# The first two blocks of modulation columns: all of them on TensorE in four banks, instead of three quarters on TensorE and one on VectorE

## The chip, the cores and the metric

One core of a Trainium2 chip runs the whole program in one launch. The metric is the device time in microseconds (us), the median of three runs.

## The reference, cut to what matters

One transformer block over 1024 latent tokens and 256 context tokens of width 1024. Before anything else it computes the modulation from two condition vectors, and it normalizes, scales and shifts every token with it:

```
s_c, s_ctx = silu(c), silu(c_ctx)                 # two vectors of 1024
mx = split(s_c   @ w_mod + b_mod, 6)              # w_mod: 1024 x 6144
mc = split(s_ctx @ w_mod + b_mod, 6)
xn = rms_norm(x,   g) * (1 + mx[1]) + mx[0]       # shift: columns 0..1023
cn = rms_norm(ctx, g) * (1 + mc[1]) + mc[0]       # scale: columns 1024..2047
... = xn @ w_in, cn @ w_in
```

Then follow a recurrence, a neighborhood attention, the merge of both and a gated feed-forward. They use `mx[2]` to `mx[5]`, which are computed later and are not touched here. The change is about columns 0 to 2047 of `w_mod`, that is 16 blocks of 128 columns, for both vectors.

## The kernel before, in words

The program is a row of blocks: `setup_block`, `mixer_block`, `merge_block` and `ffn_block`. Each is one `nc.Block`, and at its end all engines meet, so that nothing of the mixer, not even a transfer, starts before the last engine has left the setup.

Everything is kept with features on the 128 partitions: token data `xs[128, 8, 1280]`, eight chunks k of 128 features by 1280 tokens. The setup does the following.

- **SyncE** (the queue SP) issues the transfers in one written order: small ones, then the sixteen transfers of the tokens, then eight pieces of `w_mod` (`load_wm(k)`, L188, 128 x 1536 numbers each, into a ring of four, so that piece k waits for `wm_used` of piece k-4), among which stand the silu source `sr` (L196), four row blocks `load_rows(b)` (L193, ring of two) and weight tiles `raw` (L203, L205, L211, L214). The last two `raw` loads wait for `w_lo`.
- **VectorE** adds the squares of the tokens (L352), then (L354) takes them off TensorE's sums; GpSimd raises them to the power -0.5 (L223); three small operations on VectorE (L358 to L360) finish 1/rms and signal `rstd_done`.
- **TensorE** sums the squares (L232), and then computes the columns: `columns(k)` (L236 to L241) multiplies chunk k of the silu vectors `sv` (2 stationary columns) with three pieces of 512 columns, and accumulates over the eight k in three PSUM banks. After `columns(1)` it waits for `rstd_done` and spreads 1/rms over the partitions by ten transposes (L248, signal `spread`). After `columns(7)` ScalarE copies the two rows of results to `mrow` (L287), and TensorE turns them to 12 columns (L253, signal `mod_cols`).
- The three pieces are columns 0 to 511 of the shift and all 1024 of the scale. The other 512 columns of the shift are **row dots**: `shift_dots(b)` (L315, L317) on VectorE multiplies 128 transposed rows of `w_mod` by the silu vectors, which lie spread over all partitions in `sr` (loaded spread by L196, silu on ScalarE by L281), and sums along the row. The four calls stand between the steps of 1/rms, the four `normalize(k)` (L328, which waits for `spread`) and two `split_low(s)` (L325). L371 adds the bias to them.
- After `mod_cols` VectorE makes the scale `gm` (L375, L376), adds the bias to the first half of the shift (L378), and then, chunk by chunk, scales and shifts the tokens (L386, L389); ScalarE makes the high part `xnh` (L291, L293, L294), VectorE the low part `xnl` (L396, L400), signal `lo_done`. TensorE follows chunk by chunk with the first matmuls of the projection (L262 to L264), fifteen for each chunk.

The lines that say what a sentence can't:

```
for k in range(KC):
    columns(k)
    if k == 1:
        pe.wait_ge(rstd_done, 1)
        ... ten transposes, then_inc(spread, 1)
pe.wait_ge(mod_copied, 1)
```

Of the kernel before, what the change touches and what calls it, by code (L numbers as in the profile page):

```python
# [9 lines left out]
ALU = mybir.AluOpType  # L10
ACT = mybir.ActivationFunctionType
AX_X = mybir.AxisListType.X

P = 128
D = 1024
KC = D // P
# [16 lines left out]
HALF = 512  # L33
# [19 lines left out]

def build(nc, xT, ctxT, svec, c_rows, w_modk, w_shiftT, w_modT, b_mod, gains, w_fm, w_qkv, lru_w, lru_p, qk_g, rpb,
          w_mix, w_ff, ffn_p, consts, outT, yr_d, yn_d, smr_d, smn_d, bias_d):
    with ExitStack() as top:
# [10 lines left out]
        mod = sbuf(top, "mod", [P, 6 * KC, 2])  # L67
# [14 lines left out]
        with ExitStack() as queries:  # L82
            qh = sbuf(queries, "qh", [P, KC, 384], F32R)
            ql = sbuf(queries, "ql", [P, KC, 384], F32R)
        setup_block(nc, sem, sbuf, psum, xT, ctxT, svec, c_rows, w_modk, w_shiftT, gains, b_mod, lru_p, consts, w_fm, w_qkv,
                    mod, bm, gain, ones, eps, lrup, decay, xnh, xnl, qh, ql, weights, banks)
# [19 lines left out]
SEGS = ((0, C), (C, C + HALF), (C + HALF, N))  # L106
MOD_COLS = 1536
MOD_RING = 4
ROW_BLOCKS = 4
SCALED_EARLY = 4  # L110


def setup_block(nc, sem, sbuf, psum, xT, ctxT, svec, c_rows, w_modk, w_shiftT, gains, b_mod, lru_p, consts, w_fm, w_qkv,
                mod, bm, gain, ones, eps, lrup, decay, xnh, xnl, qh, ql, weights, banks):
# [5 lines left out]
    with ExitStack() as st:  # L120
# [3 lines left out]
        total = sbuf(st, "total", [P, N])  # L124
        rows = sbuf(st, "rows", [P, 2, D])
        product = sbuf(st, "product", [P, D])
        sv = sbuf(st, "sv", [P, KC, 2])
        sr = sbuf(st, "sr", [P, 2, D])
        dots = sbuf(st, "dots", [P, ROW_BLOCKS, 2])
        gm = sbuf(st, "gm", [P, 2, KC])  # L130
        la = sbuf(st, "la", [P, 6, 2, KC])
        ident = sbuf(st, "ident", [P, P])
        mrow = sbuf(st, "mrow", [P, 3, HALF])
        rms = sbuf(st, "rms", [P, 3, TB])
# [3 lines left out]
        ga = acc[:, 3, :]  # L138
        gf = gf[:, :]
        mt = ga[:, 0:24].rearrange("p (n w) -> p n w", w=2)  # L140
        ss = gf[:, 0:TB]
        rs = lower[:, 0:N]

        small_in = sem("a_small_in")
        sr_in = sem("a_sr_in")
        x_in = [sem(f"a_x_in{k}") for k in range(KC)]
        wm_in = [sem(f"a_wm_in{s}") for s in range(MOD_RING)]
        wm_used = sem("a_wm_used")
        rows_in = [sem(f"a_rows_in{s}") for s in range(2)]
        rows_used = sem("a_rows_used")  # L150
        memset_done = sem("a_memset")
        silu_done = sem("a_silu")
        sr_done = sem("a_sr_done")
        squared = sem("a_squared")
# [18 lines left out]
        with nc.Block() as block:  # L173
            @block.sync
            def _(sp):
                sp.dma_start(sv[:, :, :], svec).then_inc(small_in, 16)
                sp.dma_start(bm[:, :], b_mod).then_inc(small_in, 16)
                sp.dma_start(gain[:, :, :], gains).then_inc(small_in, 16)
                sp.dma_start(lrup[:, :, :], lru_p).then_inc(small_in, 16)
                sp.dma_start(ident[:, :], consts[:, 0:P]).then_inc(small_in, 16)  # L180
                for k in range(KC):
                    sp.dma_start(xs[:, k, 0:C], ctxT[k]).then_inc(x_in[k], 16)
                    sp.dma_start(xs[:, k, C:N], xT[k]).then_inc(x_in[k], 16)

                def load_wm(k):
                    if k >= MOD_RING:
                        sp.wait_ge(wm_used, k - MOD_RING + 1)
                    sp.dma_start(wm[:, k % MOD_RING, :], w_modk[k]).then_inc(wm_in[k % MOD_RING], 16)  # L188

                def load_rows(b):  # L190
                    if b >= 2:
                        sp.wait_ge(rows_used, b - 1)
                    sp.dma_start(rows[:, b % 2, :], w_shiftT[b]).then_inc(rows_in[b % 2], 16)  # L193

                load_wm(0)
                sp.dma_start(sr[:, :, :], bass.AP(tensor=c_rows.tensor, offset=0, ap=[[0, P], [D, 2], [1, D]]))\  # L196
                  .then_inc(sr_in, 16)
                load_wm(1)
                load_rows(0)
                load_wm(2)  # L200
                load_rows(1)
                load_wm(3)
                sp.dma_start(raw[:, 0, :], w_fm[0, :, 0:1024]).then_inc(raw_in[0], 16)  # L203
                load_wm(4)
                sp.dma_start(raw[:, 1, :], w_fm[0, :, 1024:2048]).then_inc(raw_in[1], 16)  # L205
                load_wm(5)
                load_rows(2)
                load_wm(6)
                load_rows(3)
                load_wm(7)  # L210
                sp.dma_start(raw[:, 2, :], w_qkv[0, :, 2048:3072]).then_inc(raw_in[2], 16)  # L211
                for s in range(2):
                    sp.wait_ge(w_lo, s + 1)
                    sp.dma_start(raw[:, s, :], w_qkv[0, :, 1024 * s:1024 * s + 1024]).then_inc(raw_in[s], 16)  # L214
# [12 lines left out]
            def _(pe):  # L227
# [8 lines left out]
                def columns(k):  # L236
                    pe.wait_ge(wm_in[k % MOD_RING], (k // MOD_RING + 1) * 16)
                    for n in range(3):
                        last = pe.matmul(acc[0:2, n, :], sv[:, k, :], wm[:, k % MOD_RING, HALF * n:HALF * n + HALF],
                                         start=(k == 0), stop=(k == KC - 1))  # L240
                    last.then_inc(wm_used, 1)  # L241
# [9 lines left out]
                pe.wait_ge(mod_copied, 1)  # L251
                for n in range(12):
                    last = pe.transpose(mt[:, n, :], mrow[0:2, n // 4, P * (n % 4):P * (n % 4) + P], ident[0:2, 0:2])  # L253
# [13 lines left out]
            def _(act):  # L267
# [4 lines left out]
                for k in range(KC):  # L272
# [6 lines left out]
                    act.activation(sq[:, k % 2, :], xs[:, k, :], ACT.Square).then_inc(squared, 1)  # L279
                act.wait_ge(sr_in, 16)  # L280
                act.activation(sr[:, :, :], sr[:, :, :], ACT.Silu).then_inc(sr_done, 1)  # L281
                for s in range(2):
# [3 lines left out]
                act.wait_ge(wm_used, KC)  # L286
                act.copy(mrow[0:2, :, :], acc[0:2, 0:3, :]).then_inc(mod_copied, 1)  # L287
                for k in range(KC):
# [12 lines left out]
            def _(dve):  # L301
                steps = [0]

                def then(ins):

                    steps[0] += 1
                    ins.then_inc(dve_step, 1)
                    dve.wait_ge(dve_step, steps[0])

                def shift_dots(b):  # L310

                    dve.wait_ge(rows_in[b % 2], (b // 2 + 1) * 16)
                    if b == 0:
                        dve.wait_ge(sr_done, 1)
                    dve.tensor_tensor_reduce(out=product[:, :], in0=rows[:, b % 2, :], in1=sr[:, 0, :], scale=1.0,  # L315
                                             scalar=0.0, op0=ALU.mult, op1=ALU.add, accum_out=dots[:, b, 0:1])
                    dve.tensor_tensor_reduce(out=rows[:, b % 2, :], in0=rows[:, b % 2, :], in1=sr[:, 1, :],  # L317
                                             scale=1.0, scalar=0.0, op0=ALU.mult, op1=ALU.add,
                                             accum_out=dots[:, b, 1:2]).then_inc(rows_used, 1)
                    dve.wait_ge(rows_used, b + 1)  # L320

# [26 lines left out]
                for k in range(1, KC):  # L348
                    dve.wait_ge(squared, k + 1)
                    if k >= 2:  # L350
# [3 lines left out]
                dve.tensor_scalar(rms[:, 0, :], ss, 1.0 / D, EPS, ALU.mult, ALU.add).then_inc(mean_square, 1)  # L354
                shift_dots(0)
                dve.wait_ge(root_done, 1)
# [3 lines left out]
                dve.scalar_tensor_tensor(r, w, 1.5, r, ALU.add, ALU.mult).then_inc(rstd_done, 1)  # L360
                shift_dots(1)
                dve.wait_ge(spread, 1)
# [3 lines left out]
                split_low(1)  # L366
                shift_dots(2)
                normalize(2)
                shift_dots(3)
                normalize(3)  # L370
                then(dve.tensor_tensor(mod[:, 4:KC, :], dots[:, :, :],  # L371
                                       bm[:, 4:KC].unsqueeze(2).broadcast_to([P, 4, 2]), ALU.add))
                dve.wait_ge(mod_cols, 1)
                for w in range(2):
                    then(dve.tensor_tensor(gm[:, w, :], mt[:, 4:12, w], bm[:, KC:2 * KC], ALU.add))  # L375
                    then(dve.scalar_tensor_tensor(gm[:, w, :], gm[:, w, :], 1.0, gain[:, 0, :],  # L376
                                                  ALU.add, ALU.mult))
                then(dve.tensor_tensor(mod[:, 0:4, :], mt[:, 0:4, :],  # L378
                                       bm[:, 0:4].unsqueeze(2).broadcast_to([P, 4, 2]), ALU.add))

# [1676 lines left out]
```

## Time and profile before

| | |
|---|---|
| runs | 2293.88, 2295.71, 2296.64 us; median 2295.71 |
| the profiled execution, its own time | 2292.44 us |
| its span | 2290.7 us, 29048 instructions |
| TensorE matmul busy | 2152.3 us (94%) |
| VectorE busy | 1407.6 us (61%) |
| ScalarE busy | 955.9 us (42%) |
| GpSimd busy | 263.7 us (12%) |
| mean bandwidth to and from HBM | 74 GB/s |

The profile shows one execution. The span is the time between the first and the last instruction that it shows; 1.74 us of the execution's own time lie around it. An f32 matmul is shown as two records (an instruction with 512 columns stands there twice), an fp32r one as one. The engine names are PE (matmul), PEld (weight load), DVE (VectorE), ACT (ScalarE), POOL (GpSimd) and SP (SyncE), and SPq is the issuing of a transfer on SP.

### The profile page before, as it was taken

What the parts mean: (1) busy time and instruction counts of PE and PEld (TensorE: products, weight loads), DVE (VectorE), ACT (ScalarE), POOL (GpSimd) and SP (SyncE); (2) the same over time, 40 slices, a digit from 0 to 9 for tenths busy, and PEclk for the clock granted to TensorE, in tenths of its full rate; (3) what the DMA queues carried; (4) which work ended last, traced back from release to release, by engine and by line L of the source; (5) the groups of instructions that cost most, each with busy time, mean ns of one, the idle gap of its engine ahead of it and who ended that gap; (6) DMA issues with size and microseconds to landing.
All of it is one profiled execution on the core that took longest, in us unless ns stands there. A gap on an engine that the chain in (4) does not pass through costs nothing. (4 is left out here: it accounts for less than half of the span.)

```text
span 2290.7 us, 29048 instructions
## 1 busy us (share of the span) xinstructions
PE 2152.3 (94%) x10958; PEld 1824.1 (80%) x10958; DVE 1407.6 (61%) x2572; ACT 955.9 (42%) x1472; POOL 263.7 (12%) x202
## 2 busy tenths in 40 slices
PE   5988999999999999999987799997999999999999
PEld 1877888978789788897876688875888888888887
DVE  6678587775886858768578446657554244424442
ACT  3556655665657556566557210104221022212220
POOL 0031222112212113022221100000000000000000
PEclk9999999999999999999999899998999999999999
DMA  7411212011120111111102544421221111111112
GB/s 305 119 46 36 67 38 77 28 38 59 46 68 19 54 60 37 38 58 49 56 19 88 207 165 139 152 91 69 73 70 58 48 46 53 47 55 47 53 48 99
DMA packets 68632, 167.56 MB, mean 73 GB/s; under 512 B 22704, under 2 KB 28208, under 8 KB 68400
## 3 DMA queue, kind: packets, MB, share of 16 engines
q1 hardware_dynamic: 47520, 145.20, 18.6%
q0 software_dynamic: 4608, 16.78, 2.1%
q10 hardware_dynamic: 16400, 4.19, 0.9%
q8 instruction: 66, 1.08, 0.2%
q14 instruction: 38, 0.31, 0.0%
HBM read 145.17 MB, written 25.17 MB: 74 GB/s over the span
## 5 line engine op out<-in xcount | busy, mean ns | idle before, releaser
L48 PE MATMUL t_o_ps<-qh,xnh 128*128 128x384 f32 (+1 forms) x640 | 223.5, 349 | 0.3 <-PEq L173 0.3
L50 PE MATMUL t_o_ps<-qh,xnl 128*128 128x384 f32 (+1 forms) x640 | 207.6, 324 | 0.0
L49 PE MATMUL t_o_ps<-ql,xnh 128*128 128x384 f32 (+1 forms) x640 | 207.6, 324 | 0.0
L1383 DVE TENSOR_TENSOR probT_low<-t_o_ps,probT_high 128x512 fp32r<-128x512 f32 (+2 forms) x256 | 138.9, 584 | 64.8 <-ACT probT_high L1086 64.1
L806 PE MATMUL f_ps<-xnh,wh 128*128 128x512 f32 x360 | 151.5, 421 | 11.8 <-DVE wl L1214 9.3
L1086 ACT CAST probT_high<-t_o_ps 128x512 fp32r<-128x512 f32 (+2 forms) x256 | 117.0, 510 | 92.3 <-PE t_o_ps L897 71.2
L1843 ACT CAST wh<-raw 128x1024 fp32r<-128x1024 f32 x68 | 70.9, 1044 | 192.0 <-PE pd L50 170.1
L807 PE MATMUL f_ps<-xnl,wh 128*128 128x512 f32 x360 | 143.1, 397 | 0.0
L808 PE MATMUL f_ps<-xnh,wl 128*128 128x512 f32 x360 | 143.0, 397 | 0.0
L50 PE MATMUL pg<-yh,wl 128*128 128x512 f32 x352 | 137.0, 389 | 0.0
L49 PE MATMUL pg<-yl,wh 128*128 128x512 f32 x352 | 137.0, 389 | 0.0
L48 PE MATMUL pg<-yh,wh 128*128 128x512 f32 x352 | 137.0, 389 | 0.0
L50 PE MATMUL pa<-yh,wl 128*128 128x512 f32 x336 | 130.8, 389 | 0.0
L48 PE MATMUL pa<-yh,wh 128*128 128x512 f32 x336 | 130.8, 389 | 0.0
L49 PE MATMUL pa<-yl,wh 128*128 128x512 f32 x336 | 130.8, 389 | 0.0
L1076 ACT ACTIVATE prob<-prob,stat 128x768 f32<-128x768 f32 (+1 forms) x128 | 128.1, 1001 | 3.8 <-DVE stat L1378 3.8
L1965 DVE SCALAR_TENSOR_TENSOR x<-pd,mod,x 128x512 f32 (+1 forms) x48 | 35.8, 750 | 151.3 <-PE pd L50 146.6
L48 PEld LDWEIGHTS t_o_ps<-qh,xnh 128*128 128x128 f32 x640 | 120.8, 189 | 9.0 <-issue 8.3
L49 PEld LDWEIGHTS t_o_ps<-ql,xnh 128*128 128x128 f32 x640 | 120.8, 189 | 8.3 <-issue 7.6
L1257 DVE TENSOR_REDUCE ssq<-sqs 128x4 f32<-128x256 f32 (+1 forms) x80 | 31.0, 389 | 150.0 <-ACT sqs L1032 149.7
L50 PEld LDWEIGHTS t_o_ps<-qh,xnl 128*128 128x128 f32 x640 | 120.7, 189 | 0.0
L48 PE MATMUL pd<-hh_d,wh 128*128 128x512 f32 x308 | 119.9, 389 | 0.0
(311 smaller groups left out, 5640.6 us busy)
## 6 DMA issues: line engine op xcount, KB each, us to landing
raw<-w_ff SPq DMA_DIRECT2D x68, 512.0 KB, 3.2
raw<-w_fm SPq DMA_DIRECT2D x32, 512.0 KB, 6.5
raw<-w_qkv SPq DMA_DIRECT2D x24, 512.0 KB, 3.6
raw<-w_mix SPq DMA_DIRECT2D x24, 512.0 KB, 4.4
bias<-bias_d SPq DMA_DIRECT2D x16, 448.0 KB, 5.7
wm<-w_modk SPq DMA_DIRECT2D x8, 768.0 KB, 7.7
row_c<-w_modT SPq DMA_DIRECT2D x12, 512.0 KB, 3.2
raw<-w_modT SPq DMA_DIRECT2D x12, 512.0 KB, 3.3
```

Of the source, the lines that this page charges most:

```text
L48: pe.matmul(out, w_hi(k), x_hi(k), start=(k == 0), stop=False)
L49: pe.matmul(out, w_hi(k), x_lo(k), start=False, stop=False)
L50: last = pe.matmul(out, w_lo(k), x_hi(k), start=False, stop=(k == chunks - 1))
L806: pe.matmul(out, fh[:, s, k, :], xnh[:, k, c0:c1], start=(k == 0), stop=False)
L807: pe.matmul(out, fh[:, s, k, :], xnl[:, k, c0:c1], start=False, stop=False)
L808: return pe.matmul(out, fl[:, s, k, :], xnh[:, k, c0:c1], start=False, stop=(k == KC - 1))
L1076: act.activation(p, p, ACT.Exp, bias=stat[:, u, 1:2], scale=-1.0, accum_out=stat[:, u, 2:3]).then_inc(exp_done, 1)
L1086: act.copy(probT_blocks(pth, u, bank), probT_bank(u, bank)).then_inc(pt_hi, 1)
L1257: dve.tensor_reduce(ssq[:, s, g0:4], sqs[:, s % 2, HD * g0:256].rearrange("p (g f) -> p g f", f=HD), AX_X, ALU.add).then_inc(sq_used, 1)
L1383: dve.tensor_tensor(probT_blocks(ptl, u, bank), probT_bank(u, bank), probT_blocks(pth, u, bank).bitcast(F32), ALU.subtract).then_inc(pt_lo, 1)
L1843: act.copy(flat(wh, b), raw[:, b, :]).then_inc(w_hi, 1)
L1965: dve.scalar_tensor_tensor(out, pd[:, 2 * b + half, :], mod[:, bass.ds(m + 5 * KC, 1), 0:1].rearrange("p a b -> p (a b)"), out, ALU.mult, ...
```

## The change

All 2048 columns of the two blocks go through TensorE. A piece of `w_mod` is 128 x 2048 numbers, `columns(k)` has four matmuls into four banks, `mrow` has four rows of 512, there are 16 transposes, and they go to another bank (the one of the sums of squares). The row dots, their four transfers, the spread silu source, its transfer and its silu on ScalarE, and L371 are gone. On the host, `w_modk` is a plain slice and `w_shiftT` is no more.

```diff
-MOD_COLS = 1536
+MOD_COLS = 2048
 MOD_RING = 4
-ROW_BLOCKS = 4
...
-        mrow = sbuf(st, "mrow", [P, 3, HALF])
+        mrow = sbuf(st, "mrow", [P, 4, HALF])
...
-        mt = ga[:, 0:24].rearrange("p (n w) -> p n w", w=2)
+        mt = gf[:, 64:96].rearrange("p (n w) -> p n w", w=2)
...
                 load_wm(0)
-                sp.dma_start(sr[:, :, :], bass.AP(tensor=c_rows.tensor, offset=0, ap=[[0, P], [D, 2], [1, D]]))\
-                  .then_inc(sr_in, 16)
                 load_wm(1)
-                load_rows(0)
                 load_wm(2)
-                load_rows(1)
                 load_wm(3)
                 sp.dma_start(raw[:, 0, :], w_fm[0, :, 0:1024]).then_inc(raw_in[0], 16)
                 load_wm(4)
                 sp.dma_start(raw[:, 1, :], w_fm[0, :, 1024:2048]).then_inc(raw_in[1], 16)
                 load_wm(5)
-                load_rows(2)
                 load_wm(6)
-                load_rows(3)
                 load_wm(7)
...
                     pe.wait_ge(wm_in[k % MOD_RING], (k // MOD_RING + 1) * 16)
-                    for n in range(3):
+                    for n in range(4):
...
                 pe.wait_ge(mod_copied, 1)
-                for n in range(12):
+                for n in range(16):
...
-                act.wait_ge(sr_in, 16)
-                act.activation(sr[:, :, :], sr[:, :, :], ACT.Silu).then_inc(sr_done, 1)
...
-                act.copy(mrow[0:2, :, :], acc[0:2, 0:3, :]).then_inc(mod_copied, 1)
+                act.copy(mrow[0:2, :, :], acc[0:2, :, :]).then_inc(mod_copied, 1)
...
-                shift_dots(0)
                 dve.wait_ge(root_done, 1)
...
                 dve.scalar_tensor_tensor(r, w, 1.5, r, ALU.add, ALU.mult).then_inc(rstd_done, 1)
-                shift_dots(1)
                 dve.wait_ge(spread, 1)
                 normalize(0)
                 split_low(0)
                 normalize(1)
                 split_low(1)
-                shift_dots(2)
                 normalize(2)
-                shift_dots(3)
                 normalize(3)
-                then(dve.tensor_tensor(mod[:, 4:KC, :], dots[:, :, :],
-                                       bm[:, 4:KC].unsqueeze(2).broadcast_to([P, 4, 2]), ALU.add))
                 dve.wait_ge(mod_cols, 1)
                 for w in range(2):
-                    then(dve.tensor_tensor(gm[:, w, :], mt[:, 4:12, w], bm[:, KC:2 * KC], ALU.add))
+                    then(dve.tensor_tensor(gm[:, w, :], mt[:, 8:16, w], bm[:, KC:2 * KC], ALU.add))
...
-                then(dve.tensor_tensor(mod[:, 0:4, :], mt[:, 0:4, :],
-                                       bm[:, 0:4].unsqueeze(2).broadcast_to([P, 4, 2]), ALU.add))
+                then(dve.tensor_tensor(mod[:, 0:KC, :], mt[:, 0:KC, :],
+                                       bm[:, 0:KC].unsqueeze(2).broadcast_to([P, KC, 2]), ALU.add))
```

## Rows read from the trace of the kernel before

**Rows 1.** The page: busy time of the engines over the whole span
```profile
PE 2152.3 (94%) x10958; PEld 1824.1 (80%) x10958; DVE 1407.6 (61%) x2572; ACT 955.9 (42%) x1472; POOL 263.7 (12%) x202
```
**Rows 2.** Waits, 0 to 60 us: who waited for whom, total, times, longest
```profile
ACT mrow L287 <- PE s_ps L239: 12.3, 1, 12.3
...
DVE gm L375 <- PE s_ps L253: 4.6, 1, 4.6
```
**Rows 3.** Timeline: start, length, engine, operation; TensorE from the sums on
```profile
27.49 7.73 PE L239 MATMUL s_ps<-wm,sv 128*2 128x512 f32 x12
...
29.16 0.13 PEld L239 LDWEIGHTS s_ps<-wm,sv 128*2 128x2 f32 x1 [0.73 <-issue]
30.01 0.13 PEld L239 LDWEIGHTS s_ps<-wm,sv 128*2 128x2 f32 x1 [0.73 <-issue]
...
35.15 1.31 PE L248 MATMUL t_o_ps<-ident,rms 128*128 128x128 f32 x10
...
36.38 15.61 PE L239 MATMUL s_ps<-wm,sv 128*2 128x512 f32 x36
```
**Rows 4.** The same timeline: from the end of the columns to the first projection
```profile
52.03 1.43 ACT L287 COPY mrow<-s_ps 2x1536 f32<-2x1536 f32 x1 [12.28 <-PE s_ps L239]
...
53.52 0.90 PE L253 MATMUL s_ps<-ident,mrow 2*128 2x2 f32 x12 [1.52 <-ACT mrow L287]
54.52 0.17 DVE L375 TENSOR_TENSOR gm<-s_ps,bm 128x8 f32<-128x8 f32 x1 [4.61 <-PE s_ps L253]
...
59.63 0.55 PE L262 MATMUL s_ps<-xnh,wh 128*128 128x256 f32 x1 [5.21 <-DVE xnl L396]
```
**Rows 5.** Timeline of VectorE: 1/rms, the first normalize, the last step before `mod_cols`
```profile
31.30 0.17 DVE L360 SCALAR_TENSOR_TENSOR rms<-rms 128x10 f32<-128x10 f32 x1
...
36.56 1.49 DVE L328 TENSOR_TENSOR xs<-xs,t_o_ps 128x1280 f32<-128x1280 f32 x1 [2.80 <-PE t_o_ps L248]
38.08 1.23 DVE L325 TENSOR_TENSOR wl<-raw,wh 128x1024 fp32r<-128x1024 f32 x1
...
49.75 0.17 DVE L371 TENSOR_TENSOR mod<-dots,bm 128x8 f32<-128x8 f32 x1
```
**Rows 6.** Timeline: the mixer's first matmul, and what released it
```profile
86.56 0.36 PE L48 MATMUL t_o_ps<-qh,xnh 128*128 128x256 f32 x1 [0.30 <-PEq L173]
```
**Rows 7.** Groups by line and shape, 0 to 60 us: busy us, mean ns, idle before
```profile
L291 ACT CAST xnh<-xs 128x1280 fp32r<-128x1280 f32 x2 | 2.4, 1257 | 3.2 <-DVE xs L386 3.2
L284 ACT CAST wh<-raw 128x1024 fp32r<-128x1024 f32 x2 | 2.1, 1045 | 11.3 <-DMA raw<-w_fm 11.3
```
**Rows 8.** The same groups: the row dots and the spread silu
```profile
L315 DVE CUSTOM_DVE_ANT_0 product<-rows,sr 128x1024 f32<-128x1024 f32 x4 | 4.9, 1222 | 0.0
L317 DVE CUSTOM_DVE_ANT_0 rows<-rows,sr 128x1024 f32<-128x1024 f32 x4 | 4.9, 1220 | 0.0
...
L281 ACT ACTIVATE sr<-sr 128x2048 f32<-128x2048 f32 x1 | 1.9, 1910 | 1.8 <-DMA sr<-c_rows 1.8
```
**Rows 9.** Timeline of SP: when transfers of the ring are issued
```profile
32.67 0.33 SPq L188 DMA_DIRECT2D wm<-w_modk  x1
...
42.10 0.43 SPq L211 DMA_DIRECT2D raw<-w_qkv  x1
42.57 1.04 SPq L214 DMA_DIRECT2D raw<-w_qkv  x2
```
**Rows 10.** Stretch: length, busy PE, PEld, DVE, ACT, POOL, PEclk, DMA share, GB/s
```profile
44.00:48.00 4.00, 4.00 (x11) 0.80 (x10) 3.93 (x6) 0.00 (x0) 0.00 (x0) 1.00 1.02 421
```
**Rows 11.** Stretches by L262 alone: first two chunks of the projection, length first
```profile
59.60:64.42 4.82, 2.67 (x6) 1.65 (x6) 0.64 0.01 3
64.42:67.50 3.08, 1.84 (x5) 0.94 (x5) 1.00 0.00 0
```
**Rows 12.** Timeline: distance of fp32r matmuls of 512 columns in the projection
```profile
65.00 0.39 PE L263 MATMUL s_ps<-xnl,wh 128*128 128x512 f32 x1
65.23 0.39 PE L264 MATMUL s_ps<-xnh,wl 128*128 128x512 f32 x1
```

More of the change, by code:

```diff
@@ L51, in three_passes, with build @@
     return last
-def build(nc, xT, ctxT, svec, c_rows, w_modk, w_shiftT, w_modT, b_mod, gains, w_fm, w_qkv, lru_w, lru_p, qk_g, rpb,
+def build(nc, xT, ctxT, svec, c_rows, w_modk, w_modT, b_mod, gains, w_fm, w_qkv, lru_w, lru_p, qk_g, rpb,
           w_mix, w_ff, ffn_p, consts, outT, yr_d, yn_d, smr_d, smn_d, bias_d):
@@ L84, in build @@
             ql = sbuf(queries, "ql", [P, KC, 384], F32R)
-        setup_block(nc, sem, sbuf, psum, xT, ctxT, svec, c_rows, w_modk, w_shiftT, gains, b_mod, lru_p, consts, w_fm, w_qkv,
+        setup_block(nc, sem, sbuf, psum, xT, ctxT, svec, c_rows, w_modk, gains, b_mod, lru_p, consts, w_fm, w_qkv,
                     mod, bm, gain, ones, eps, lrup, decay, xnh, xnl, qh, ql, weights, banks)
@@ L106, with setup_block @@
 SEGS = ((0, C), (C, C + HALF), (C + HALF, N))
-MOD_COLS = 1536
+MOD_COLS = 2048
 MOD_RING = 4
-ROW_BLOCKS = 4
 SCALED_EARLY = 4
-def setup_block(nc, sem, sbuf, psum, xT, ctxT, svec, c_rows, w_modk, w_shiftT, gains, b_mod, lru_p, consts, w_fm, w_qkv,
+def setup_block(nc, sem, sbuf, psum, xT, ctxT, svec, c_rows, w_modk, gains, b_mod, lru_p, consts, w_fm, w_qkv,
                 mod, bm, gain, ones, eps, lrup, decay, xnh, xnl, qh, ql, weights, banks):
@@ L124, in setup_block @@
         total = sbuf(st, "total", [P, N])
-        rows = sbuf(st, "rows", [P, 2, D])
-        product = sbuf(st, "product", [P, D])
         sv = sbuf(st, "sv", [P, KC, 2])
-        sr = sbuf(st, "sr", [P, 2, D])
-        dots = sbuf(st, "dots", [P, ROW_BLOCKS, 2])
         gm = sbuf(st, "gm", [P, 2, KC])
@@ L144, in setup_block @@
         small_in = sem("a_small_in")
-        sr_in = sem("a_sr_in")
         x_in = [sem(f"a_x_in{k}") for k in range(KC)]
@@ L148, in setup_block @@
         wm_used = sem("a_wm_used")
-        rows_in = [sem(f"a_rows_in{s}") for s in range(2)]
-        rows_used = sem("a_rows_used")
         memset_done = sem("a_memset")
         silu_done = sem("a_silu")
-        sr_done = sem("a_sr_done")
         squared = sem("a_squared")
@@ L188, in load_wm @@
                     sp.dma_start(wm[:, k % MOD_RING, :], w_modk[k]).then_inc(wm_in[k % MOD_RING], 16)
[L190 to L193, printed above, removed]
                 load_wm(0)
-                sp.dma_start(sr[:, :, :], bass.AP(tensor=c_rows.tensor, offset=0, ap=[[0, P], [D, 2], [1, D]]))\
-                  .then_inc(sr_in, 16)
                 load_wm(1)
-                load_rows(0)
                 load_wm(2)
-                load_rows(1)
                 load_wm(3)
@@ L308, in then @@
                     dve.wait_ge(dve_step, steps[0])
[L310 to L320, printed above, removed]
                 def split_low(s):
@@ L2035 @@
         "svec": np.stack([cols(a["c"][0]), cols(a["c_ctx"])], 2),
-        "c_rows": np.stack([a["c"][0], a["c_ctx"]]), "w_modk": np.concatenate([a["w_mod"][0][:, 0:HALF], a["w_mod"][0][:, D:2 * D]], 1).reshape(KC, P, MOD_COLS),
-        "w_shiftT": a["w_mod"][0][:, HALF:D].T.reshape(ROW_BLOCKS, P, D),
+        "c_rows": np.stack([a["c"][0], a["c_ctx"]]), "w_modk": a["w_mod"][0][:, 0:MOD_COLS].reshape(KC, P, MOD_COLS),
         "w_modT": a["w_mod"][0][:, 2 * D:].T.reshape(4 * KC, P, D), "b_mod": cols(a["b_mod"][0]),
```

## The prediction

> **What bounds the kernel now.** I read the busy times first: TensorE is busy for 94% of the span and no other engine for more than 61% [rows 1]. So work that is added to TensorE costs its length wherever TensorE is what the others wait for, and work that is taken from VectorE gives nothing there. That is an average over stages, and the change lies in the first 60 us; the second view is therefore the list of waits of this stretch. The longest waits after the token sums point one way: ScalarE's copy to `mrow` stood 12.3 us waiting for the columns, and VectorE's first operation on them, L375, stood 4.6 us waiting for the transposes [rows 2]. The third view, the timeline, gives the path that sets the end of the setup: columns from 27.49 us, ten transposes at 35.15, columns again from 36.38 for 15.61 us [rows 3], the copy at 52.03, the turning at 53.52, VectorE at 54.52, the projection at 59.63, after 5.2 us of waiting for the first chunk of tokens, which itself waits for the columns [rows 4]. VectorE had ended its last work before that, L371, at 49.75 + 0.17 = 49.92 us [rows 5]: it had 4.6 us to spare. Last, the mixer's first matmul comes at 86.56 us, released by the end of the block (L173) [rows 6], where all engines meet. Whatever delays the columns delays the whole rest by the same.
>
> **What the change costs on that path.**
> *The matmuls.* Eight chunks get one f32 matmul of 512 columns more, 16 records. In the second stretch 36 records take 15.61 us, 0.434 each with the last one's tail, so I take 0.43 [rows 3]. In the first chunk the distance of two weight loads is 30.01 - 29.16 = 0.85 us, twice that: TensorE then runs at the lower of its two levels. The first twelve records take 7.66 us (27.49 to 35.15) [rows 3]; with s slow ones 0.85s + 0.43(12 - s) = 7.66, so s is about 6. The start at 27.49 hangs on the token sums, which the change leaves alone, so I let the slow stretch be as long in time as before: six records slow in either kernel. The first two chunks then take 7.66 + 4 x 0.43 = 9.4 us and the others 12 x 0.43 = 5.2 us more than before: together **+6.9 us**. Bounds: below, no f32 record stands closer than 0.43 (what if one could is rival 2); above, all 16 at 0.85 would be 13.6, but when twelve of them come the stream has long been fast, so I take as the upper end that the four of the first two chunks are slow, 6.9 + 4 x 0.42 = 8.6.
>
> That the price per matmul is the moving columns' and not an overlap that a fourth bank would fill rests on that row alone. The Trainium skill, "TensorE: Matmul & The Clock Gate", section "Back-to-back issue gap", gives some 131 ns as the sustained distance of matmuls of 512 columns, and "FP8 and Floating Point Precision" counts four passes for true FP32: by these an instruction would be 0.52 us, the eight would cost 4.2 us, and the sum below would be 4.9. The trace disagrees: 0.87 us for an instruction of two records.
>
> *ScalarE's copy* has 2048 instead of 1536 numbers in a row. A cast of 1280 takes 1.257 us and one of 1024 1.045 [rows 7], 0.83 ns a number, so 512 more are **+0.43**. The nearest bound above is in proportion, 1.43/3 = 0.48 [rows 4]; below I see 0.35 if a fixed part is larger than it seems. It lies on the path.
>
> *The turning.* Twelve transposes take 0.90 us [rows 4], four more about a third of it less the fixed part, **+0.25** (0.2 to 0.3). That they go to the bank of the sums of squares costs nothing: VectorE has read them before it makes 1/rms, and the projection writes it only after VectorE has read the columns.
>
> *VectorE after them.* L378 has 16 numbers instead of 8. Its like L375 takes 0.17 us with 8 [rows 4]; between nothing and in proportion (0.17) I take **+0.02**, since so short an operation is nearly all fixed time. L375 and L376 stay.
>
> Sum on the path: 6.9 + 0.43 + 0.25 + 0.02 = **+7.6 us**.
>
> **What is removed, and why it gives nothing.** The row dots are 4 x 1.222 + 4 x 1.220 = 9.8 us on VectorE, with the reads of their accumulators and L371 some 10.6 [rows 8]. The first call runs while GpSimd makes the root; without it VectorE waits for the root at the same time as before. 1/rms would be ready at 31.5 us as before [rows 5], but TensorE asks for it only after two chunks, now at 27.49 + 9.4 = 36.9 instead of 35.15. So `spread` and the first `normalize` come 1.7 us *later*, at 38.3. Then four normalizes (1.49) and two splits (1.23) [rows 5] end at about 38.3 + 8.4 = 46.7, if the second weight tile is there; `mod_cols` comes at about 54.4 + 7.6 = 62.0. VectorE's spare time grows from 4.6 to some 15 us. The silu on ScalarE, 1.9 us and its table [rows 8], stands between the squares and a cast of a weight tile that stood waiting for its transfer (L284, 11.3 us in two waits [rows 7]): also beside the path. If these covers were gone, the removed work would be worth those 10.6 us; nothing is near it.
>
> **The queue and the transfers.** Gone are the spread source (1.0 MB) and four row blocks (2.1 MB), added is 8 x 0.26 = 2.1 MB. Before 27 us the tokens' transfers stand first in the queue, so the start does not move. The ring: piece 4 can be issued when the first chunk is used, at 27.5 + 6 x 0.85 + 2 x 0.43 = 33.4 instead of 32.67 [rows 9], piece 5 at 36.9, 6 at 41.5, 7 at 44.9. TensorE wants piece 4 at 44.9 (two chunks of 3.44 us after the transposes' end at 38.1) and piece 7 at 55.2, 10.3 us after its issue. Behind piece 7 three weight tiles are issued at once (0.52 MB each) [rows 9]; even if all share the 421 GB/s that this time shows [rows 10], 2.6 MB are in after 6.2 us, and 4 us are left for the way there. So the ring costs nothing. What waits behind the later `load_wm` on SP are those three tiles; ScalarE wants them only after all token chunks, so behind 59.63 [rows 4]. The chunk loop after `mod_cols` is the same work with the same data and shifts whole.
>
> **The rivals.**
> 1. *The clock.* TensorE rests while the copy and the first chunk are made, and comes back slow: the first chunk of the projection takes 4.82 us at a granted 0.64, the next 3.08 at 1.00 [rows 11], so this drop costs 1.7 us; the slow start at 27.49 costs 6 x 0.42 = 2.5. If the rise comes at another moment of the stream, either can be smaller or larger: the sum becomes 7.6 - 4.2 = +3.4 at the least, and as far the other way 7.6 + 4.2 = +11.8, that is 2299.1 to 2307.5. For it speaks that these rows show both levels; against it, that start and gaps are the same in both kernels and a median over runs meets the same lottery: the runs before lie within 2.8 us. The Trainium skill, "TensorE: Matmul & The Clock Gate", section "What's actually happening", says that the number of slow matmuls at a start differs from run to run, 6, 11 or 14 in one kernel; no run here shows that yet. Chance 0.12, half of it small enough for "within 0.2%".
> 2. *The fourth matmul is partly free*, because matmuls into one more bank overlap more. The shortest distance that rows show for 512 columns is that of fp32r ones in the projection, 65.23 - 65.00 = 0.23 us [rows 12]; at that distance 16 records are 3.7 us, and the sum is 3.7 + 0.7 = +4.4, 2300.1. Against it: 36 f32 records, over three banks, without a hole at 0.43. The rule of the Trainium skill quoted above (TensorE: Matmul & The Clock Gate) points this way, and the row speaks against it. Chance 0.02.
> 3. *Vector work was the real bound* (faster). If the dots delayed what TensorE or ScalarE waits for, 10.6 us go and only the copy and the turning (+0.7) come: -9.9 us, 2285.8. It decides from the point where VectorE's last operation before L375 ends after `mod_cols`; the trace has it 4.6 us ahead. The same sign, smaller, if the columns started earlier for the 1 MB less in the queue; but they start behind the token sums. Chance 0.02.
> 4. *The ring starves TensorE.* A piece is a third larger and three tiles share its way. If pieces 4 to 7 came 1 us late each, +4 to the sum, +11.6, 2307.3, just outside the range. It decides from 10.3 us between issue and landing. Chance 0.04.
> 5. *The edit gives no change*, some wait in the mixer swallowing the shift. Its engines all start together, so there is no slack to swallow it: 2295.7. Chance 0.02.
>
> **How the numbers follow.** The profiled execution took 2292.44 us (span 2290.7, 1.74 around it), so with the change it would take 2300.0. It was the fastest one shown; the median is 3.27 us above it, and the same sum against the median gives 2295.71 + 7.6 = **2303.3 us**, +0.33%. My forecast has a chance of 0.78. A measurement of this kernel can tell 0.2% from no change, 4.6 us. "Within" gets half of rival 1, rivals 2 and 5 in part, and the forecast's own scatter: 0.11; faster 0.02; slower 0.87. The range goes down to +3.8 and up to +11.3, nearly the ends of rival 1, with the bounds of the terms inside: 2299.5 to 2307.0.
>
> **What would show it.** In the profile after: 64 records of L239 at 0.43 us; transposes L248 at about 36.9; the copy at about 58.9 with 1.86 us; 16 transposes in 1.15 to 1.2; L375 at about 62.1 with a wait of 14 to 16 us on TensorE; the first L262 at about 67.2, the mixer at 94.1. The prediction is wrong if the copy starts before 57 or after 61, if TensorE waits for a transfer of `wm`, or if the mixer's start has moved by 7.6 us and the end has not.

## The result, and the profile after

The changed kernel takes **2302.07 us** (median of nine runs, 2300.78 to 2303.53), the kernel before 2294.38 us in as many (2293.64 to 2296.64): +7.7 us, a ratio of 1.0031 with an interval of 1.0022 to 1.0041, so clearly slower, by 5 to 9 us. The forecast was +7.6 us; the 2303.3 us are 1.2 us too high, since the median of three runs that they start from was itself 1.3 us above that of nine.

The busy times of the page after. TensorE has 8 us more, VectorE 11 us less, ScalarE 2 us less [rows 1]:

```profile
PE 2160.4 (94%) x10978; PEld 1827.4 (79%) x10978; DVE 1396.5 (61%) x2555; ACT 953.8 (41%) x1470; POOL 262.1 (11%) x202
```

The waits of the first 70 us after (who waited for whom, total, times, longest). The copy waits 18.1 us for the columns instead of 12.3, VectorE 15.5 us for the turning instead of 4.6 [rows 2]. All that VectorE no longer has to do has become waiting:

```profile
ACT mrow L265 <- PE s_ps L219: 18.1, 1, 18.1
...
DVE gm L335 <- PE f_ps L233: 15.5, 1, 15.5
DVE xs L294 <- PE t_o_ps L228: 6.6, 1, 6.6
```

The path after, in the timeline (start, length, engine, operation), to lay beside [rows 3], [rows 4] and [rows 6]:

```profile
27.09 8.34 PE L219 MATMUL s_ps<-wm,sv 128*2 128x512 f32 x16
35.37 1.31 PE L228 MATMUL t_o_ps<-ident,rms 128*128 128x128 f32 x10
36.60 20.76 PE L219 MATMUL s_ps<-wm,sv 128*2 128x512 f32 x48
...
57.40 1.85 ACT L265 COPY mrow<-s_ps 2x2048 f32<-2x2048 f32 x1 [18.07 <-PE s_ps L219]
...
59.31 1.15 PE L233 MATMUL f_ps<-ident,mrow 2*128 2x2 f32 x16 [1.95 <-ACT mrow L265]
60.56 0.17 DVE L335 TENSOR_TENSOR gm<-f_ps,bm 128x8 f32<-128x8 f32 x1 [15.53 <-PE f_ps L233]
...
65.68 0.55 PE L242 MATMUL s_ps<-xnh,wh 128*128 128x256 f32 x1 [5.22 <-DVE xnl L356]
...
93.32 0.33 SPq L588 DMA_DIRECT2D cst<-consts  x1
```

48 records take 20.76 us where 36 took 15.61, 0.43 each in both. The mixer's first transfer, the end of the setup, is at 93.32 us. In the kernel before it is 6.8 us earlier:

```profile
86.51 0.33 SPq L628 DMA_DIRECT2D cst<-consts  x1
```

### The profile page after: what moved, and what is told of

It is laid out like the page before. It is cut to its first block and busy times, and to the rows that moved or that the text cites. A ratio compares the mean times of both kernels' runs of the same rounds, so it can differ in the third digit from the quotient of the medians.

```text
span 2299.0 us, 29060 instructions
## 1 busy us (share of the span) xinstructions
PE 2160.4 (94%) x10978; PEld 1827.4 (79%) x10978; DVE 1396.5 (61%) x2555; ACT 953.8 (41%) x1470; POOL 262.1 (11%) x202
```

## The experiments

All kernels keep the mixer and everything behind it. "Rest" below is the time from the mixer's first transfer to the end of the span. The medians of the kernel before beside the first four kernels (23 runs) and beside the others (27 runs) are 2294.87 and 2295.18 us. The changed kernel did not run beside them; where a kernel is compared with it, its 2302.07 us are meant. The kernel before had 2294.38 us then, so such a difference is uncertain by some 0.8 us more. Each start time comes from one trace of its kernel.

| kernel | time, us | ratio to before (interval) | copy starts | first scale operation | mixer starts | rest |
|---|---|---|---|---|---|---|
| before, first trace | 2294.38 | | 52.03 | 54.52 | 86.51 | 2204.2 |
| before, second trace | 2296.0 (one run) | | 51.73 | 54.21 | 86.34 | 2207.9 |
| changed | 2302.07 | 1.0031 (1.0022 to 1.0041) | 57.40 | 60.56 | 93.32 | 2205.7 |
| e1: removal alone | 2295.4 | 1.0003 (0.9994 to 1.0012) | 51.42 | 53.91 | 85.91 | 2207.8 |
| e2: fourth matmul alone | 2301.98 | 1.0031 (1.0020 to 1.0042) | 58.57 | 61.06 | 93.17 | 2207.5 |
| e3: fifth matmul | 2309.8 | 1.0065 (1.0051 to 1.0079) | 64.53 | 67.69 | 100.50 | 2209.2 |
| e4: two matmuls | 2291.03 | 0.9983 (0.9974 to 0.9992) | 47.36 | 49.42 | 81.60 | 2209.0 |
| e5: two matmuls, removal | 2289.16 | 0.9975 (0.9966 to 0.9984) | 45.45 | 47.52 | 80.60 | 2206.8 |
| e6: early columns | 2295.88 | 1.0001 (0.9992 to 1.0010) | 51.24 | 54.41 | 86.38 | 2208.2 |
| e7: early, split copy | 2293.65 | 0.9995 (0.9986 to 1.0004) | 48.49 | 52.47 | 84.67 | 2207.8 |

### The removal alone

```diff
 # on the kernel before, three matmuls a chunk
-                load_rows(0)
...
-                load_rows(3)
...
-                act.wait_ge(sr_in, 16)
-                act.activation(sr[:, :, :], sr[:, :, :], ACT.Silu).then_inc(sr_done, 1)
...
-                shift_dots(0)
...
-                shift_dots(3)
...
-                then(dve.tensor_tensor(mod[:, 4:KC, :], dots[:, :, :],
-                                       bm[:, 4:KC].unsqueeze(2).broadcast_to([P, 4, 2]), ALU.add))
+                then(dve.tensor_copy(mod[:, 4:KC, :], bm[:, 4:KC].unsqueeze(2).broadcast_to([P, 4, 2])))
```

(The transfer that loads `sr` is gone too.)

Expected:

> The kernel before with its three matmuls per chunk, and only what the change removes is gone: the row dots, the spread silu, and their five transfers (so 512 columns of the shift are their bias alone). My theory (TensorE's columns set the end of the setup, the removed work lies beside them): the copy to mrow starts within 0.5 us of 52.0 us, and the time is the same, 0 to -0.5 us. Rival, vector work was the real bound: -9.9 us. Rival, the transfers held the tokens: the first matmul of the columns comes earlier by as much as the time falls, about 0.4 us as in the changed kernel's trace.

Measured: 2295.4 us, a ratio of 1.0003 (0.9994 to 1.0012): no change that can be told, while -9.9 us would be a ratio of 0.9957. VectorE's spare time in front of the turned columns doubled, and that is all that the removal gave. The timeline of its VectorE says it (L362 is the first scale operation, L375 in the kernel before):

```profile
44.23 0.17 DVE L359 COPY mod<-bm 128x8 f32<-128x8 f32 x1
...
53.91 0.17 DVE L362 TENSOR_TENSOR gm<-s_ps,bm 128x8 f32<-128x8 f32 x1 [9.50 <-PE s_ps L247]
```

The copy started at 51.42 us, 0.6 before the expected 52.0 and so a little outside the 0.5 us that I had allowed. It is where the stream began: the sums of squares started at 22.57 us here and at 23.16 in the first trace of before. That is not the missing transfers: with all of before's transfers they started at 22.59 us in the next kernel, e2, and at 22.58 us in the second trace of before.

### The addition alone

```diff
 # on the kernel before; the fourth bank is read by nobody
-                    for n in range(3):
-                        last = pe.matmul(acc[0:2, n, :], sv[:, k, :], wm[:, k % MOD_RING, HALF * n:HALF * n + HALF],
+                    for n in range(4):
+                        c = HALF * (n % 3)
+                        last = pe.matmul(acc[0:2, n, :], sv[:, k, :], wm[:, k % MOD_RING, c:c + HALF],
```

(The turned columns move to the other bank, as in the change.) Expected:

> The kernel before with its row dots, and a fourth matmul in every chunk that repeats the first piece into a fourth bank nobody reads; copy, turning and transfers are as before. My theory: 16 records at 0.43 us, +6.9 us (5.9 to 7.7 by when the clock rises). Rival, a matmul into one more bank is partly free: +3.7 us. Rival, the removed work had hidden a gain, so the addition alone costs more than the change did: over +8.5 us.

Measured: 2301.98 us, +7.1 us over the 2294.87 us beside it. The +3.7 us of a partly free matmul would be a ratio of 1.0016, below the interval of 1.0020 to 1.0042, and the timeline of TensorE has the price of the record directly:

```profile
26.91 9.69 PE L240 MATMUL s_ps<-wm,sv 128*2 128x512 f32 x16
36.53 1.30 PE L249 MATMUL t_o_ps<-ident,rms 128*128 128x128 f32 x10
37.77 20.76 PE L240 MATMUL s_ps<-wm,sv 128*2 128x512 f32 x48
```

The 48 records take the same 20.76 us as in the changed kernel, with row dots on VectorE and four more transfers beside them. So the two parts add up: nothing that can be told from the removal, and the matmuls' price from the addition. The longer copy and turning of the change (0.67 us together) are not in this kernel; they are below what these times can tell, and are read from the traces.

### A fifth matmul

```diff
 # on the changed kernel
                     for n in range(4):
+                        if n == 3:
+                            pe.matmul(acc[0:2, n, :], sv[:, k, :], wm[:, k % MOD_RING, HALF * n:HALF * n + HALF],
+                                      start=(k == 0), stop=False)
                         last = pe.matmul(acc[0:2, n, :], sv[:, k, :], wm[:, k % MOD_RING, HALF * n:HALF * n + HALF],
-                                         start=(k == 0), stop=(k == KC - 1))
+                                         start=(k == 0 and n < 3), stop=(k == KC - 1))
```

Expected:

> The changed kernel with a fifth matmul in every chunk, the fourth one done twice into its bank (so 512 columns of the scale are doubled). My theory: +6.9 us over the changed kernel, +14.6 over the kernel before, since the columns are still what all wait for. Rival, partly free: +3.7 over the changed one. Rival, the transfers of the ring had paced the changed kernel: 0 to +2 over it.

Measured: 2309.8 us, +7.7 us over the changed kernel and +14.9 us over the kernel before it ran beside. The time is a line in the number of matmuls: three, four, five give about 2295, 2302 and 2310. In the trace the mixer starts 7.2 us later than in the changed kernel. One chunk's columns from the timeline, ten records in 49.74 - 45.45 = 4.29 us:

```profile
45.45 1.02 PE L220 MATMUL s_ps<-wm,sv 128*2 128x512 f32 x2
46.30 3.60 PE L222 MATMUL s_ps<-wm,sv 128*2 128x512 f32 x8
...
49.74 1.02 PE L220 MATMUL s_ps<-wm,sv 128*2 128x512 f32 x2
```

### Two matmuls: where the line ends

```diff
 # on the kernel before
-                    for n in range(3):
+                    for n in range(2):
...
-                    last = pe.transpose(mt[:, n, :], mrow[0:2, n // 4, P * (n % 4):P * (n % 4) + P], ident[0:2, 0:2])
+                    last = pe.transpose(mt[:, n, :], mrow[0:2, n // 4 % 2, P * (n % 4):P * (n % 4) + P], ident[0:2, 0:2])
...
-                act.copy(mrow[0:2, :, :], acc[0:2, 0:3, :]).then_inc(mod_copied, 1)
+                act.copy(mrow[0:2, 0:2, :], acc[0:2, 0:2, :]).then_inc(mod_copied, 1)
```

Expected:

> The kernel before with two matmuls per chunk (512 columns of the scale are copies of others), row dots and transfers as before; copy and turning have a third less. My theory: TensorE's side of the path falls by 6.9 + 0.4 = 7.3 us, but VectorE had 4.6 us to spare in front of the turned columns, and its normalize starts up to 1.7 us earlier, so the time falls by 4.6 to 6.3 us and VectorE becomes what is late. Rival, vector work was the bound already: 0 us. Rival, VectorE's row dots were no cover at all: -7.3 us.

Measured: 2291.03 us, -3.8 us, short of the 4.6 to 6.3 us of my theory, though its interval (-1.8 to -6.0 us) does not exclude it. The first scale operation came 4.8 to 5.1 us before that of the two traces of before, which is inside my range, but for another reason than mine. I had named VectorE as what would be late, and it was not: L375 still waited 0.93 us for TensorE.

```profile
48.33 0.17 DVE L371 TENSOR_TENSOR mod<-dots,bm 128x8 f32<-128x8 f32 x1
49.42 0.17 DVE L375 TENSOR_TENSOR gm<-s_ps,bm 128x8 f32<-128x8 f32 x1 [0.93 <-PE s_ps L253]
```

TensorE had run out of pieces of `w_mod`:

```profile
33.84 7.27 PE L239 MATMUL s_ps<-wm,sv 128*2 128x512 f32 x16
42.29 1.88 PE L239 MATMUL s_ps<-wm,sv 128*2 128x512 f32 x4 [1.17 <-DMA wm<-w_modk]
45.45 1.88 PE L239 MATMUL s_ps<-wm,sv 128*2 128x512 f32 x4 [1.28 <-DMA wm<-w_modk]
```

Without these two waits, 2.45 us, TensorE would have been the earlier one, and VectorE late after all: only 0.9 us more could be had. My estimate of why the pieces are late: a chunk of two matmuls takes 4 x 0.43 = 1.72 us, and what lies in the ring's way for it (a piece of 0.79 MB and a row block or a weight tile of 0.52) takes 3.1 us at the 421 GB/s of [rows 10]. With three matmuls (2.6 us) the four pieces of the ring still cover that, and no trace with three shows a wait for a piece; with two they do not. To see whether it is the transfers, the removal went on top of it: the same edit as in e1, on e4. Expected:

> The kernel with two matmuls per chunk (e4_two), and the row dots, the spread silu and their transfers taken out as well. In e4_two TensorE waited 1.17 and 1.28 us for pieces of w_mod. If the transfers in the ring's way had become the bound there, both waits go or shrink and L375's successor starts about 2.4 us earlier, at 46.5 to 47.5 us instead of 49.4, and the time falls 1.5 to 2.5 us below e4_two. Rival, VectorE's row dots held it (L375 had waited 0.93 us only): the waits for w_mod stay, and nothing or under 1 us is won.

Measured: 2289.16 us, 6.0 us below the kernel before in its company, where e4 was 3.8 below. The intervals of the two overlap, so the rows decide: the first scale operation is at 47.52, where e4 has 49.42. The waits for pieces, by the list of waits of 0 to 60 us, shrank without going (e5; e4 had 2.5 in two):

```profile
DVE gm L362 <- PE s_ps L247: 5.3, 1, 5.3
...
PE s_ps L233 <- DMA wm<-w_modk: 1.1, 2, 0.7
```

The 1.4 us of shorter waits and a start 0.6 us earlier make up the 1.9 us of the first scale operation. The dots and the transfers left together, so this kernel alone doesn't tell them apart; the rows of e4 do, where TensorE waits for pieces and VectorE waits for TensorE, with 0.93 us to spare.

### The changed kernel in a better order

In the changed kernel TensorE did nothing until 22.8 us, and VectorE waited 15.5 us. Since only the end of the columns counts, they can begin before the tokens are there:

```diff
 # on the changed kernel; load_x(k) is the two transfers of a token chunk
-                for k in range(KC):
+                def load_x(k):
                     sp.dma_start(xs[:, k, 0:C], ctxT[k]).then_inc(x_in[k], 16)
                     sp.dma_start(xs[:, k, C:N], xT[k]).then_inc(x_in[k], 16)
...
                 load_wm(0)
                 load_wm(1)
-                load_wm(2)
-                load_wm(3)
+                for k in range(4):
+                    load_x(2 * k)
+                    load_x(2 * k + 1)
+                    load_wm(2 + k)
+                load_wm(6)
                 sp.dma_start(raw[:, 0, :], w_fm[0, :, 0:1024]).then_inc(raw_in[0], 16)
-                load_wm(4)
+                load_wm(7)
                 sp.dma_start(raw[:, 1, :], w_fm[0, :, 1024:2048]).then_inc(raw_in[1], 16)
-                load_wm(5)
-                load_wm(6)
-                load_wm(7)
...
-                pe.wait_ge(summed, KC - 1)
-                for b in range(TB):
-                    last = pe.matmul(ss[:, b:b + 1], total[:, P * b:P * b + P], ones[:, 0:1], start=True, stop=True)
-                last.then_inc(mean_done, 1)
...
                 for k in range(KC):
                     columns(k)
+                    if k == 4:
+                        pe.wait_ge(summed, KC - 1)
+                        for b in range(TB):
+                            last = pe.matmul(ss[:, b:b + 1], total[:, P * b:P * b + P], ones[:, 0:1], start=True, stop=True)
+                        last.then_inc(mean_done, 1)
-                    if k == 1:
+                    if k == 5:
                         pe.wait_ge(rstd_done, 1)
```

Expected:

> The changed kernel with another order: the first two pieces of w_mod are loaded ahead of the tokens, the next four between pairs of token chunks, the last two after them; TensorE does five chunks of columns before it sums the squares, and spreads 1/rms after the sixth. Nothing is computed otherwise. In the changed kernel TensorE stood idle until 22.8 us and VectorE had 15.5 us to spare. My theory (the end of the columns alone sets the end of the setup): the copy starts at about 47.5 us instead of 57.4, the first scale operation at about 51, and the time is some 9 us below the changed kernel and 2 us below the kernel before. Rival, the tokens come so late that the row of 1/rms, normalize and split becomes the bound: the first scale operation waits for nothing of TensorE, and the time is that of the kernel before or above. Rival, the transfers pace the columns: waits of TensorE for pieces of w_mod, the copy after 52 us.

Measured: 2295.88 us, 6.2 us below the changed kernel (7.0 if each is set against the kernel before beside it; 9 were expected) and not to be told from the kernel before. The path was the columns still (the first scale operation waited 1.80 us for TensorE), but they ended at 51.2 us and not at 47.5:

```profile
22.06 3.60 PE L216 MATMUL s_ps<-wm,sv 128*2 128x512 f32 x8 [1.58 <-DMA wm<-w_modk]
27.70 5.29 PE L216 MATMUL s_ps<-wm,sv 128*2 128x512 f32 x8 [2.04 <-DMA wm<-w_modk]
33.76 2.77 PE L225 MATMUL f_ps<-ones,total 128*128 128x1 f32 x20 [0.77 <-DVE total L320]
36.46 6.55 PE L216 MATMUL s_ps<-wm,sv 128*2 128x512 f32 x8
```

At the higher level eight records take 3.44 us. After the sums of squares eight of them, without a wait, take 6.5 us (36.46 to 42.94), so some seven ran at 0.85; the profile's granted clock for 37 to 40 us is 0.50. That cost about 3 us of the 3.7 that the columns ended late; where the other 0.7 lies is not shown.

The chunk at 27.70 was slow too, by 1.7 us, but that cost nothing: after it TensorE still waited 0.77 us for VectorE's sum (L320), which waits for the tokens. The trace of the next kernel, e7, with the same order, shows it. There the same chunk ran fast, the wait after it was longer, and the sums started at the same time:

```profile
27.63 3.60 PE L217 MATMUL s_ps<-wm,sv 128*2 128x512 f32 x8 [2.04 <-DMA wm<-w_modk]
33.64 3.96 PE L228 MATMUL f_ps<-ones,total 128*128 128x1 f32 x20 [2.42 <-DVE total L328]
37.53 5.30 PE L217 MATMUL s_ps<-wm,sv 128*2 128x512 f32 x8
```

So the same hole of 2.04 us was followed by slow records in one trace (granted clock 0.61 from 28.0 to 31.5) and by fast ones in the other (1.00). In both the records after the sums were slow, and from the start of the sums to the transposes it took 9.2 and 9.1 us. A stream that starts early but with holes gives back at the clock a part of what it wins, here some 3 of 9 us.

The last kernel splits the copy:

```diff
 # on e6
-                act.copy(mrow[0:2, :, :], acc[0:2, :, :]).then_inc(mod_copied, 1)
+                for n in range(4):
+                    if n < 3:
+                        act.wait_ge(bank_done, n + 1)
+                    else:
+                        act.wait_ge(wm_used, KC)
+                    act.copy(mrow[0:2, n, :], acc[0:2, n, :]).then_inc(mod_copied, 1)
```

(`bank_done` is signalled by the matmuls of chunk 7; TensorE turns the four columns of a bank as soon as it is copied.) Expected:

> e6_early with the copy to mrow made bank by bank, each as soon as its last matmul is done, and the transposes of a bank as soon as it is copied. The copy stands on the path with 1.85 us and the turning with 1.15: the last bank's copy is about 0.6 us, the last four transposes 0.3, so the first scale operation comes 1.9 us earlier than in e6_early. Rival, each short copy has a fixed part that eats it: under 0.8 us earlier. A difference in the time of this size is at the edge of what five rounds tell; the trace decides.

Measured: 2293.65 us, 2.2 us less than e6. The intervals of the two overlap; the traces have the first scale operation 1.94 us earlier, as expected. The four copies take 0.57 us each and three of them hide behind the last matmuls:

```profile
48.49 0.57 ACT L275 COPY mrow<-s_ps 2x512 f32<-2x512 f32 x1 [6.81 <-PE s_ps L217]
...
51.07 0.58 ACT L275 COPY mrow<-s_ps 2x512 f32<-2x512 f32 x1 [0.28 <-PE s_ps L217]
```

Now the other side is level: VectorE takes up the columns at once after its last normalize, without a wait.

```profile
49.44 3.00 DVE L304 TENSOR_TENSOR xs<-xs,t_o_ps 128x1280 f32<-128x1280 f32 x2
52.47 0.17 DVE L345 TENSOR_TENSOR gm<-f_ps,bm 128x8 f32<-128x8 f32 x1
```

So all 2048 columns on TensorE can be had at the time of the kernel before (0.9986 to 1.0004 of it), 8.4 us below the change as it was made (8.3 if each is set against the kernel before beside it). That it beats the kernel before is not shown.

### How much a single trace says

Expected of the kernel before, run once more:

> The kernel before, unchanged, for a second trace. From the mixer's start to the end of the span five traces so far show 2204.2 to 2209.2 us, in kernels whose mixer and later blocks are the same. If that scatter belongs to the single execution, this trace will not repeat the 2204.2 of the first one of this kernel but lie at 2206 to 2209, with its setup within 1 us of the first (mixer at 85.8 to 87.2 us). Rival, the changes in the setup carry over into later stages: 2204.2 within 0.5 us.

Measured: 2296.0 us, mixer at 86.34 us, rest 2207.9. The setup repeats within 0.3 us, the rest does not, by 3.7 us. So the "+8.3 us" between the two spans (2290.7 and 2299.0) is 6.8 of setup and 1.5 of scatter in stages that the change does not touch.

## Why the prediction was right

It is a sum on one path, and each term can be read off. The path and what lies beside it were right. That +7.6 and the measured +7.7 us lie within 0.1 is luck: the interval is 5.0 to 9.4 us, and in the traces the mixer starts 6.8 us later than in the first one of before and 7.0 later than in the second. In that sum the matmuls cost 1.1 us less than forecast, 0.4 us came from an earlier start, and 0.7 us came on top that the forecast had not counted.

**The matmuls, +6.9.** The sixteen records cost 0.43 each: from 36.60 on, twelve more cost 5.15 us (forecast 5.2). The first two chunks cost 0.62 us more (35.37 - 27.09 against 35.15 - 27.49) where I had 1.72, because of the clock: by the step used there, (8.28 - 16 x 0.43)/0.42, some 3.3 records were slow and not 6. That is rival 1, on its small side, 1.1 us. The same step gives 5.9 and 6.6 for the two traces of before, 5.9 in e1, 6.5 in e2, 3.6 in e3, 4.8 in e4, 5.6 in e5, that is 1.4 us from end to end. Neither the removal alone (5.9) nor the fourth matmul alone (6.5) makes the number small. The two kernels with both (3.3 and 3.6) have the smallest ones, in one trace each, so whether this is the execution or the change is open. I had quoted the Trainium skill, "TensorE: Matmul & The Clock Gate", section "What's actually happening", that the number of slow matmuls at a start differs from run to run. The two traces of the one kernel before differ too, by 0.7 of a record only.

**The copy, +0.43, and the turning, +0.25.** Measured +0.42 (1.85 against 1.43) and +0.25 (1.15 against 0.90). The copy started at 57.4 and not at 58.9: 1.1 us of clock, and 0.4 us because the sums had started earlier (22.77 us against 23.16). This is scatter: the second trace of before has 22.58.

**After them.** From the first scale operation to the first projection 5.12 us against 5.11; L338 with 16 numbers takes the 0.17 us of one with 8, so the 0.02 was nothing. The first chunk of the projection was 0.7 us longer (5.52 us to the next at 71.20, against 4.79), again at the slow level: the profile's stretch 65.7 to 69.1 has a granted clock of 0.50. So the mixer came at 93.3 where 94.1 was forecast: -1.5 and +0.7.

**What is removed gives nothing.** Shown by e1: the lower end of its interval, 0.9994, leaves room for a gain of 1.4 us at most. The transposes for `spread` started 0.2 us later than before and not 1.7, by the clock (1.1) and the earlier start (0.4), and the normalizes and splits ended at 45.0 us (46.7 forecast), 15.5 us ahead.

**The ring costs nothing.** Right for the change: TensorE waits for no piece, and the last one was issued at about 43.7 us (44.9 forecast). But rival 4 looked for the danger in the wrong place. It is on the other side: fewer matmuls a chunk, not bigger pieces (e4).

**The rivals.** The partly free fourth matmul (2) is refuted by e2 and e3: 0.43 us a record with three, four and five matmuls a chunk. An f32 instruction of 512 columns costs twice 0.43 us. The sustained distance of 131 ns that the Trainium skill gives ("TensorE: Matmul & The Clock Gate", section "Back-to-back issue gap") is not borne out for these instructions. Vector work as the bound (3) is refuted by e1. The swallowed shift (5) by the medians. The fallacy would have been to read the 10.6 us taken from VectorE as a gain to set against 6.9: none of them was ever on the path.

## What to carry to other kernels

Before work is moved from one engine to another, ask which of the two the next step waits for. Here VectorE had 4.6 us to spare with the row dots in place, so the quarter of the columns that it took was free, and from three to five matmuls a chunk each one on TensorE cost its full 0.86 us a chunk. A second quarter on VectorE (10.6 us by the first) would not have fitted into 4.6. And cover has an end on the transfer side too: with a third of TensorE's work gone, it was the ring of loads that was late, with VectorE 0.9 us behind it.

## What the runs showed of the hardware that I had not expected

GpSimd's root of 128 x 10 numbers (L223, L203) takes 2.87 us beside a row dot of VectorE and 1.98 us without one. The removal alone is enough for it. Timelines of GpSimd, the addition alone (with dots) and the removal alone:

```profile
27.35 2.87 POOL L223 TENSOR_TENSOR rms<-rms,power_a 128x10 f32<-128x10 f32 x1 [26.33 <-DVE rms L355]
```

```profile
27.32 1.98 POOL L217 TENSOR_TENSOR rms<-rms,power_a 128x10 f32<-128x10 f32 x1 [26.30 <-DVE rms L346]
```

The prediction had taken the root's time as the same. The 0.9 us cost nothing: 1/rms was ready at 30.1 us after and at 31.5 before, and TensorE asked for it only at 35. The Trainium skill, "SBUF — State Buffer", section "Who interferes with whom", has VectorE and GpSimd share a pair of ports, which only one of them holds at a time; a row dot reads two operands from SBUF, and the longer root agrees with it in its direction. The dot itself took its 1.22 us. What part of the 0.9 us is the ports was not tried.

The profile's granted clock reads 1.00 in the first slow stretch, where the distance of the records says 1.2 GHz (the lower level): the stretch 27.10 to 30.10 us after, with five matmul records started, against 0.50 in the second one. Columns: stretch, length, busy PE, PEld, DVE, ACT, POOL, clock, DMA share, GB/s.

```profile
27.10:30.10 3.00, 3.00 (x5) 0.46 (x5) 0.67 (x4) 0.00 (x0) 1.98 (x1) 1.00 0.85 355
...
65.70:69.10 3.40, 3.40 (x10) 2.82 (x11) 3.40 (x6) 1.29 (x2) 0.00 (x0) 0.50 0.00 0
```

In e6 the column does read 0.50 at the slow records after the sums. So for the first stream of an execution the distance of the weight loads is the clock to read, and not that column.
